# Seven edits to the order of work in a single-core Trainium2 kernel of two transformer-like blocks

## What is computed

```python
# first block
x = x + rglru_layer(x)              # projections, causal conv of width 4, gated linear recurrence, out projection
k_nope, k_rope, v = mla_shared_kv(x)
x = x + mla_layer(x)                # latent attention, 8 heads, causal, gated by silu(gate)
x = rms_norm(x)
# second block
q, k, v, g_a, z, xbc, dt = split(rmsnorm(x) @ w_in)
y_a = rmsnorm(diff_attention(q, k, v)) * silu(g_a)       # 8 heads, each softmax(1) - lam * softmax(2), causal
y_b = rmsnorm((ssd_scan(conv(xbc), dt) + d_skip * xh) * silu(z))   # 8 chunks of 128 tokens
x = x + concat(y_a, y_b) @ w_out
q, k, v, g = split(rmsnorm(x) @ w_in_c + b_in_c)
x = x + (sliding_window_attention(q, k, v) * silu(g)) @ w_out_c    # window 128, 16 heads taken as 8 pairs
return rmsnorm(x)
```

## Time and profile before

| | us |
|---|---|
| median of 3 runs | 2458.32 |
| lowest and highest run | 2453.52, 2461.74 |
| the profiled execution, its own time | 2459.31 |
| its span, from the first to the last instruction | 2457.5 |
| PE busy in the span | 2371.7 |

### The profile page before, as it was taken

One profiled execution on the slowest core, in us unless ns is written; L12 is line 12 of the kernel. 1 busy time (PEld: TensorE's weight loads), 2 busy tenths in 40 slices (PEclk: granted clock), 3 DMA queues, 4 the chain that ended last, 5 costly groups with the idle time before them and its releaser, 6 DMA issues. The chain is left out here.

```text
span 2457.5 us, 31376 instructions
## 1 busy us (share of the span) xinstructions
PE 2371.7 (97%) x12011; PEld 1955.0 (80%) x12011; DVE 1488.4 (61%) x2742; ACT 1222.9 (50%) x2208; POOL 185.0 (8%) x112
## 2 busy tenths in 40 slices
PE   8999999998999999999999999999999999999988
PEld 6777687887888878788888887888777787888877
DVE  6767756445566657655555555553476666666665
ACT  5545633324455544566666555432445434666652
POOL 0000021000000043000000000000022130000022
PEclk9999999999999999999999999999999999999999
DMA  3222332122221332111101111224534431111143
GB/s 131 76 79 82 127 103 75 53 80 82 89 76 66 108 104 76 44 44 35 44 27 43 35 44 35 86 97 145 196 124 159 142 98 55 44 52 44 44 141 120
DMA packets 93711, 203.05 MB, mean 83 GB/s; under 512 B 10560, under 2 KB 46016, under 8 KB 92544
## 3 DMA queue, kind: packets, MB, share of 16 engines
q1 hardware_dynamic: 93280, 200.98, 24.0%
q10 hardware_dynamic: 288, 0.14, 0.0%
HBM read 160.13 MB, written 40.96 MB: 82 GB/s over the span
## 5 line engine op out<-in xcount | busy, mean ns | idle before, releaser
L224 PE MATMUL acc<-operand_hi,w_hi 128*128 128x512 f32 (+1 forms) x1814 | 728.5, 402 | 22.2 <-DVE operand_lo L516 7.7
L226 PE MATMUL acc<-operand_hi,w_lo 128*128 128x512 f32 (+1 forms) x1814 | 710.8, 392 | 0.0
L225 PE MATMUL acc<-operand_lo,w_hi 128*128 128x512 f32 (+1 forms) x1814 | 708.7, 391 | 0.0
L224 PEld LDWEIGHTS acc<-operand_hi,w_hi 128*128 128x128 f32 x1814 | 342.9, 189 | 98.7 <-issue 14.7
L226 PEld LDWEIGHTS acc<-operand_hi,w_lo 128*128 128x128 f32 x1814 | 342.3, 189 | 74.6
L225 PEld LDWEIGHTS acc<-operand_lo,w_hi 128*128 128x128 f32 x1814 | 343.1, 189 | 67.8 <-issue 3.6
L192 DVE TENSOR_TENSOR w_lo<-w_raw,w_hi 128x1024 fp32r<-128x1024 f32 (+2 forms) x201 | 225.8, 1124 | 179.6 <-ACT w_hi L186 177.4
L186 ACT ACTIVATE w_hi<-w_raw 128x1024 fp32r<-128x1024 f32 (+2 forms) x201 | 195.0, 970 | 274.4 <-PE aux L226 141.8
L224 PE MATMUL aux<-operand_hi,w_hi 128*128 128x512 f32 x618 | 252.4, 408 | 20.6 <-DVE resid L3355 5.5
L225 PE MATMUL aux<-operand_lo,w_hi 128*128 128x512 f32 x618 | 243.9, 395 | 0.0
L226 PE MATMUL aux<-operand_hi,w_lo 128*128 128x512 f32 x618 | 243.7, 394 | 0.0
(11 more groups left out here) (471 smaller groups left out, 3829.3 us busy)
## 6 DMA issues: line engine op xcount, KB each, us to landing
w_raw<-in_stream SPq DMA_DIRECT2D x199, 512.0 KB, 3.6
ssd_e<-cs_scratch SPq DMA_DIRECT2D x8, 1024.0 KB, 6.9
g_scratch<-ssd_work SPq DMA_DIRECT2D x12, 512.0 KB, 2.9
ssd_xbc<-g_scratch SPq DMA_DIRECT2D x8, 768.0 KB, 4.9
y_scratch<-rnn_y SPq DMA_DIRECT2D x10, 512.0 KB, 2.6
out_a_raw<-y_scratch SPq DMA_DIRECT2D x19, 256.0 KB, 4.7
g_scratch<-mlai_g SPq DMA_DIRECT2D x8, 512.0 KB, 2.9
mlah_g<-g_scratch SPq DMA_DIRECT2D x8, 512.0 KB, 3.7
```

Source lines behind the costliest of these rows:

```text
L224: pe.matmul(out, w_hi, x_hi, start=first, stop=False)
L225: pe.matmul(out, w_hi, x_lo, start=False, stop=False)
L226: return pe.matmul(out, w_lo, x_hi, start=False, stop=last)
```

## The change

It removes and adds almost nothing; it moves instructions in the engines' lists.

1. `begin`: the split of the second gate tile's weights stands before the copy of the factors on ACT.
2. `mla_heads`: the clearing of the mask stands behind two splits on DVE.
3. `LAST_BEFORE`: in the last differential head one unit each is taken from t = 1, 2 and 3, and one is given to t = 6 and two to t = 7.
4. `step_sizes_and_z`: the load for z6 is issued before `cs` is stored; four rows of y are loaded there, the other four after the load for z7, between the stores of z4 and z5.
5. `ssd_chunks`, DVE: in chunks 1 to 6 `added` stands before `times_gate`.
6. `ssd_chunks`, ACT, last chunk: a square root of one column, with its table load, is put before the squares, and the root before the copy of the chunk before.
7. `window_attention`: operands 0 to 3 are loaded before pair 6 is stored. In the last pair, operand 0 is split before the gate's copy and before the second weight tile, and each later operand is split one query tile earlier.

```diff
@@ -405,6 +405,7 @@
         split_hi(act, k, Tile(0, 0, 2, 1))
         stats_act(act, k, s, 0)
         ahead.exp_magnitude(act)
+        split_hi(act, k, ahead.next_gate)
         act.wait_ge(s["rb"], 1)
         act.activation(factor[:, :], rb, ACT.Copy).then_inc(s["spread"], 1)
 
@@ -1282,7 +1283,7 @@
         act.wait_ge(s["mag"], 1)
         act.activation(dw[:, 3, :], dw[:, 2, :], ACT.Exp, scale=-1.0).then_inc(s["e"], 1)
 
-    ahead.magnitude, ahead.exp_magnitude = magnitude, exp_magnitude
+    ahead.magnitude, ahead.exp_magnitude, ahead.next_gate = magnitude, exp_magnitude, g_tile(1)
 
     @block.scalar
     def _(act):
@@ -1305,7 +1306,6 @@
                 act.wait_ge(s["scan"], b)
             act.activation(thi[:, :], gates[1], ACT.Tanh, scale=0.5, bias=col("b_ig", b)).then_inc(s["thi"], 1)
 
-        split_hi(act, k, g_tile(1))
         front(0)
         for b in range(RNN_TILES):
             g = g_tile(b)
@@ -2151,9 +2151,9 @@
             dve.tensor_tensor(qa[64:128, b % 2, :], t12[head_rows(b), 0, :], as_f32(qa[0:64, b % 2, :]), ALU.subtract
                               ).then_inc(s["qal"], 1)
 
-        dve.memset(mask[:, 0:wide - P], 0.0).then_inc(s["zeros"], 1)
         split("r", 0)
         split("q", 0)
+        dve.memset(mask[:, 0:wide - P], 0.0).then_inc(s["zeros"], 1)
         split("k", 0)
         for part in range(4):
             rotate(0, part)
@@ -2224,7 +2224,7 @@
 
 UNITS_BEFORE = (0, 4, 4, 5, 4, 6, 3, 6)
 UNITS_BEHIND = (2,) * QT
-LAST_BEFORE = (0, 4, 4, 5, 2, 3, 2, 4)
+LAST_BEFORE = (0, 3, 3, 4, 2, 3, 3, 6)
 LAST_BEHIND = (2, 2, 2, 2, 0, 0, 0, 0)
 
 
@@ -2955,6 +2955,11 @@
         def tile(i, h):
             t = z_tile(i, h)
             load_ahead(sp, k, j0, 1 + h, 2, i, shift=m.shift)
+            if 2 * i + h == 4:
+                store_cs()
+            if 2 * i + h == 5:
+                for d in range(DT // 2, DT):
+                    m.load_y(sp, d)
             sp.wait_ge(k.acc_free[t.slot], t.before + 1)
             sp.dma_start(k.z_dram[bass.ds(2 * i + h, 1)].rearrange("a p c -> (a p) c"), z[:, h, :]
                          ).then_inc(s[f"stored{h}"], 16)
@@ -2964,13 +2969,13 @@
             sp.dma_start(k.cs_dram.rearrange("c (h l) -> (c h) l", l=P), cst).then_inc(s["stored"], 16)
             sp.wait_ge(s["stored"], 16)
             m.load_c(sp, 0)
-            for d in range(DT):
+            for d in range(DT // 2):
                 m.load_y(sp, d)
 
         load_ahead(sp, k, j0, 0, 2, 0, shift=m.shift)
         m.load_x(sp, 0)
         m.load_x(sp, 1)
-        rounds(tile, {3: store_cs})
+        rounds(tile, {})
         for h in range(2):
             sp.wait_ge(s[f"stored{h}"], 16 * iters)
 
@@ -3303,10 +3308,14 @@
             split_hi(act, k, tile(b + 1))
             if b < last:
                 m.decays(act, b + 1)
+            if b == last:
+                act.activation(k.small[:, 7:8], k.ones[:, 0:1], ACT.Sqrt)
             squares(b)
+            if b == last:
+                root(b)
             output(b - 1)
-            root(b)
             if b < last:
+                root(b)
                 by_token(b + 1)
         output(last)
 
@@ -3428,8 +3437,11 @@
                 m.differences(dve, b + 1)
             split_lo(dve, k, tile(b + 1))
             summed(b)
+            if b < last:
+                added(b, 0)
             times_gate(b)
-            added(b, 0)
+            if b == last:
+                added(b, 0)
             variance(b)
             if b < last:
                 m.causal(dve, b + 1)
@@ -3500,8 +3512,12 @@
                 for h in (4 + 2 * par, 5 + 2 * par):
                     load_ahead(sp, k, j0, h, per, i, shift=shift)
             p = 2 * i + par
+            if p == SW_PAIRS - 2:
+                for d in range(4):
+                    sp.wait_ge(s["stored"], 16 * d + 16)
+                    begun.load(sp, d)
             if last:
-                for d in range(SW_PAIRS - 1):
+                for d in range(4, SW_PAIRS - 1):
                     sp.wait_ge(s["stored"], 16 * d + 16)
                     begun.load(sp, d)
                 begun.load_rest(sp)
@@ -3660,16 +3676,18 @@
                 if n + 2 < QT or not last:
                     act_exp(act, p if n + 2 < QT else p + 1, (n + 2) % QT)
                 if n == 0:
+                    if last:
+                        act.wait_ge(k.tile_done[g_tile(i, par).slot], g_tile(i, par).before + 1)
+                        begun.high(act, 0)
                     act.wait_ge(s["y"], groups * p)
                     act_gate(act, g_tile(i, par), p)
                 if n == 2:
                     act_tanh(act, g_tile(i, par))
                 if last:
                     if n == 0:
-                        act.wait_ge(k.tile_done[g_tile(i, par).slot], g_tile(i, par).before + 1)
                         split_hi(act, k, begun.tile(1))
-                    if n < SW_PAIRS - 1:
-                        begun.high(act, n)
+                    if n + 1 < SW_PAIRS - 1:
+                        begun.high(act, n + 1)
                     if n == 6:
                         act.wait_ge(s["y"], ready)
                         begun.high(act, SW_PAIRS - 1, y[:, 0:HALF])
@@ -3757,9 +3775,10 @@
                 dve.scalar_tensor_tensor(out=g[:, :], in0=tg[:, :], scalar=1.0, in1=g[:, :],
                                          op0=ALU.add, op1=ALU.mult).then_inc(s["gate"], 1)
             if last and n == 0:
+                begun.low(dve, 0)
                 split_lo(dve, k, begun.tile(1))
-            if last and n < SW_PAIRS - 1:
-                begun.low(dve, n)
+            if last and n + 1 < SW_PAIRS - 1:
+                begun.low(dve, n + 1)
 
         def pair(i, par, last):
             p = 2 * i + par
```

## The result

| | before | changed |
|---|---|---|
| median, us | 2457.27 (6 runs, 2453.52 to 2461.74) | 2435.49 (6 runs, 2433.54 to 2438.02) |
| span of the profiled execution | 2457.5 | 2433.1 |
| mean granted clock | 0.987 | 0.992 |

The ratio is 0.9912, with a 95% interval of 0.99 to 0.9925: 21.6 us faster, where 21.8 had been forecast, and 2435.5 us where 2436.5 had been. So the match of the total is in part luck, and the parts are of more use than the sum.

A forecast was written before the change was run, and what follows sets the result against it. PE was taken as the bound, busy 2371.7 of 2457.5 us, so only its waits and half-clock stretches could be won: waits 15.4 plus clock 7.9, less 1.5, gives 21.8 us and a median of 2436.5, range 2430 to 2441.

The forecast's parts named there:

- The margin of 0.65 us: At the first conv tile in `begin`: the taps end at 46.9, 0.65 us before PE's tile ends at 47.55.
- The 0.7 us: In `mla_heads`: PE's wait of 2.2 us for the low weights of `r` falls to 1.5, 0.7 less.
- The term for the clock, 1.7: Behind the wait for `r` in `mla_heads`: 1.7 us gained as PE's clock stays full after the shortened wait.
- The edge between 1.71 and 2.2 us: Anywhere PE waits: the wait length above which the clock falls to 1.2 GHz lies somewhere between 1.71 and 2.2 us.
- the first rival: At the shortened waits: the waits go but the clock does not return, 15.4 us less, 2443; chance 0.18.
- as the remaining wait is short: Last differential head, t = 7: with 1.4 us of wait left, the clock gives back half of 6.14, 3.1 us.
- the prediction's own signs of being wrong: 0.50 behind waits of 1.5 us, L1262 waiting over 1 us, or the root's table load pushing the squares before PE's last product.
- The clock's 1.4: Behind the wait for z6's low weights: 2.90 busy us at half the clock shrink by 1.4.
- The 1.5 taken off the clock: Deducted from the clock's 7.9 us, about one stretch in five, for remaining waits of 1.4 and 1.5 and thin evidence.
- the four places: Taps, `r`, last differential head's last turn and z6, with 1.2 GHz behind each wait; clock terms 1.7, 1.7, 3.1, 1.4 us.
- The rival of the next wait: At the taps and z6: another wait takes the place, 11.6 of 21.8 us lost, 2448; chance 0.08.
- that of the late loads: At the first chunk: the last four y land late and its output work stands still, 2466 or more; chance 0.02.

The follow-up runs named there:

- the second pair: Both kernels run again unchanged, each for a second profile: the kernel before took 2456.66 us (ratio 1.0005), the changed kernel 2435.56 us (0.9912).

## Why the prediction was right, step by step

- **Edit 1**, forecast 7.2, measured 6.4 (interval 3.7 to 8.8). The wait went as worked out, from the copies on ACT to the taps. The margin of 0.65 us held where the tile ahead had its stretch at 1.2 GHz, as in the profile it was read from, and was used up where it had not: 0.7 to 0.8 us of wait stay then. And DVE was late once more 30 us later: 0.9 us of wait that the forecast had left out. The clock behind the taps returned in all profiles.
- **Edit 2**, forecast 2.4, with edit 6 measured 1.7 (-0.7 to 4.2). The 0.7 us is right as to its place and wrong as a gain: 0.6 came back at L1900. The term for the clock, 1.7, was taken as sure from one profile, but behind this wait the clock fell in 3 of 7, so it was worth some 0.7 on the average. The edge between 1.71 and 2.2 us that the first rival supposed is not there: waits of 2.2 us left the clock alone in 4 of 7, and a wait of 2.9 us at 889 us never did.
- **Edit 3**, forecast 4.4, measured 3.4 (1.2 to 5.7). The wait fell by 1.3 as forecast. The step that failed is "as the remaining wait is short": another of 0.7 us (L2369) stands 1.1 us behind it, and with it the clock fell in 4 of 4. Half of the stretch was won, 1.4 us and not 3.1. (A unit takes 0.68 us, not the 0.65 of the forecast: in the changed kernel one starts at 955.13 and the next at 955.81.) This is one of the prediction's own signs of being wrong, 0.50 behind a wait of some 1.5 us, and it came up here, though not at `r`.
- **Edit 4**, forecast 4.4, measured 3.2 (1.0 to 5.4). The wait of 3.0 is gone whole and the late loads of y held up nothing: no wait for them shows from 1700 to 1760 us but 0.9 for the residual, which was there. The clock's 1.4 was taken as sure in the forecast, and the clock fell in 4 of 7 profiles, for 2.9 to 6.2 us.
- **Edit 5**, forecast 2.9, measured 2.9 (0.2 to 5.7). All five waits are gone.
- **Edit 6**, forecast nothing: the wait stays at 2.6. Its time was not measured apart from edit 2's.
- **Edit 7**, forecast 2.0, measured 2.7 (0.2 to 5.2). The waits gave 1.9. That no clock returns was too careful: the stretch at 1.2 GHz is half as long in most of the profiles.

In the profiled pair the waits were forecast 2.1 us too high (15.4 against 13.3). The 0.75 left at the taps, the 0.9 at 76 us and the 0.5 at L1900, 2.2 in all, account for it. The clock was forecast 4.7 too low there, and of that some 4 us lie at places that no edit touches, so they are luck of the two executions: the profile before had 66 us at 1.2 GHz within its span and its second 59, the changed kernel 38 and 44. In the second pair the split is another. PE's busy time fell from 2369.0 to 2363.9, 5.1 us of clock, and its idle time from 85.3 to 70.2, 15.2 us of waits, 20.3 together against 24.4 in the first pair and 21.8 by the medians. So neither part is known to better than some 2 us from two profiles. They also trade with each other: where the clock is low ahead of something that comes at its own time, PE is late and waits less, as at the taps and in the last banded pair.

The first rival, that the clock does not return, came true in part at the last turn alone. The 1.5 taken off the clock was of the right kind and somewhat small: by PE's busy time at 1.2 GHz, averaged over the seven profiles without each edit and the seven with it (four for the turn), the four places gave an estimated 2.3, 0.7, 1.1 and 1.1 us, 5.2 in all where 6.4 had been counted. The rival of the next wait came true in small, at two places with 1.5 us together; that of the late loads not at all.

So the mechanism held at each place. That the total came within 0.2 us of the forecast is luck beyond that: the interval of the ratio is 18.4 to 24.6 us.

## What to carry to other kernels

A wait that is cut is worth what PE then does not wait for a few microseconds later: follow the engine that was waited for through its own list to the next thing that it gives, since it may have gained less than PE did, as at both such places here (76 us and L1900). Units of filler count only if they stand between the two events whose distance is fixed, which here were one turn and the next, and not scores and turn. What a clock stretch behind a wait is worth should be read from several profiles of the same kernel; here a wait near others, and the one above 5 us, cost it each time, single ones of 2 to 3 us sometimes or always, depending on the place, and a run of one-column matmuls without any wait each time.

## What the runs showed of the chip

The lowered clock behind a given wait is not a property of the program alone: with 3.0 to 3.2 us at z6 it fell in 4 of 7 profiles, for 3.4 to 6.8 us, and with 2.2 us at `r` in 3 of 7. At other places it is: it fell in 14 of 14 behind the 2.9 us at 889 us, and in 14 of 14 behind the 32 one-column matmuls at 967 us, where PE did not wait at all. The median of the kernel before stayed between 2456.9 and 2458.7 us over the three groups of runs; that a dozen such places average out within a run of 2.5 ms would explain it, but was not tested. A single profile can stand 3 us of span beside another (2457.5 and 2454.4) with the same waits.
